# Even block: place of the values, order of the remainders and of the raw loads; third ffn: which down tile works on which state-space table

## The chip, the cores and the metric

The kernel runs on 1 core of one Trainium2 chip. The metric is the device time of that core in microseconds (us), for one execution of the whole program. Its engines are TensorE (PE, matmuls), VectorE (DVE), ScalarE (ACT), GpSimd (POOL) and SyncE (SP, here a queue that only starts DMAs). ScalarE starts some DMAs too. Each engine runs its own instructions strictly in the order of the program, and waits at semaphores for the others.

## The reference, cut to what matters

Two layers (DEPTH 2) of a hybrid network over 256 latent tokens and 256 context tokens, model width 1024, float32. Each layer is three stages, each closed by a layer norm with a scaled residual: a half ffn (SwiGLU, hidden width 2816), a mixer, and another half ffn.

```python
for l in range(DEPTH):
    x = half_ffn(x, mod_l, 0, ffn_a, ...);  cx = half_ffn(cx, mod_c, 0, ffn_a, ...)
    if l % 2 == 0:   # [2-D neighbourhood attention | bidirectional mLSTM]
        yc, yl = even_mixer(hc @ ev_w_in[e], hl @ ev_w_in[e], ...)
    else:            # [bidirectional S5 (state space) | bidirectional retention]
        yc, yl = odd_mixer(hc @ od_w_in[e], hl @ od_w_in[e], ...)
    x = layer_norm(alpha * x + gate(mod_l, 1) * (yl @ w_out), ...)
    x = half_ffn(x, mod_l, 2, ffn_b, ...)
```

The state-space part of the odd mixer needs, from the parameters alone, for each of 8 batches (4 groups of state tiles, 2 directions): operators (small input, output and local matrices) and tables, over the chunks of time, of sine, cosine and decay.

## The kernel before

The stages are ffn0, even block, ffn1, ffn2, odd block, ffn3. "The third ffn" is ffn2. Activations lie with the feature on the partition, 8 tiles of 128 features, 512 tokens wide (256 context, then 256 latent).

**High and low parts.** Most projections are done with rounded operands in three groups of matmuls: high weights by high inputs, high weights by low inputs, and low weights by high inputs. ScalarE makes the high part (a copy that rounds), VectorE the low part or remainder (weights minus high part).

**Even block, projections.** The first four tiles (input of the convolution) are followed by 21 parts, `PARTS`: 0 to 4 are the output gate (four) and the gate rows (part 2), 5 to 8 the queries, 9 to 12 the keys, 13 to 16 the attention's values, 17 to 20 the mLSTM's values. High parts lie in two buffers (`part_hi`, part u in u % 2): `next_hi(u)` on ScalarE makes the high part of u + 2 when TensorE has done part u. `part_rest(u)` (L2267) on VectorE makes the remainder. TensorE does a part in `even_tile` (L864, L866, then L869 with the remainder) or `even_values` (L885, L886, L890).

**State-space operators in the even block.** Between the parts TensorE also works for the odd block: `turn_raw(b)` (L798) transposes raw operands of batch b behind the parts of `TURN_BEHIND`, `s5_operators(b)` (L810, L813) turns and multiplies its blocks behind the parts of `OPERATORS_BEHIND`. VectorE's `s5_operators(b)` (L2186 to L2236) builds the input block (ready at L2224, semaphore s5_blk_ready) and the output block (L2234). ScalarE's `s5_operators(b)` (L1442) issues the raw loads of batch b + 2 (`raw_in`, L1439 and L1440, two buffers), copies the results out of PSUM (L1450, L1451, L1458) and issues two stores of operators to DRAM (L1462, L1464). After every second batch VectorE sums the local matrices (`s5_local_sum`, L2250, L2253) and ScalarE stores them (`local_out`, L1469). `REST_BEFORE` says which remainders VectorE makes in front of its work on batch b. The operators' work buffers are in slot 3 (`in_out`, `pre_tmp`), in `R` (`out_blk`, `local`) and in `L`. The mLSTM's values `ml_v` lie in slot 3 over `in_out`, so ScalarE waits for all stores (semaphores s5_ops_written, s5_local_written) before it copies them there (L1555).

**The gate rows.** ScalarE's `soft_rows` (L1517 to L1521) works behind part 4; VectorE then does scans over the rows (L2302 to L2318), and only behind these `part_rest(6)`.

**Attention.** TensorE transposes the rows (L923), forms scores two tiles at a time (L940), VectorE takes maxima (L2343 to L2347), ScalarE exponentials (`exps(p)`, L1590), VectorE scales (L2358), TensorE turns the probabilities (L969), ScalarE copies them (L1601). The third and fourth buffers of probabilities lie in `R`, over `local` and `out_blk`.

**Down tiles of an ffn.** TensorE does 8 output tiles (L711, L717, L720, for each of two halves of the weights). For tile d + 1 ScalarE makes the high parts (L1295; half 0 after half 0 of tile d, half 1 after tile d), VectorE the remainders (L2071). VectorE adds the residual of tile d (L1944), ScalarE squares it (L1325), GpSimd sums both (L2557, L2563). TensorE starts tile d + 2 only after the residual of tile d. At tile 7 the context and the latent tokens are done apart, and `norm_stats` (L750 to L758) needs the sums and the last residual and square (L1965, L1346).

**Tables in the third ffn.** For table u VectorE computes phases (`phases(u)`, L1778 to L1785), ScalarE two sines (`sines(u)`, L1266, L1267), GpSimd decay and cosine (`cosines(u)`, L2681 to L2686), and ScalarE stores the table (`table_out`, L1274). Two buffers, so `phases(u)` waits for the store of table u − 2. Before, table d belongs to down tile d, and each engine does it first thing in its step d.

Of the kernel before, what the change touches and what calls it, by code (L numbers as in the profile page):

```python
# [66 lines left out]
OPERATORS_BEHIND = {7: 0, 9: 1, 11: 2, 12: 3, 14: 4, 16: 5, 17: 6, 19: 7}  # L67
REST_BEFORE = {0: (7,), 1: (8, 9), 2: (10, 11), 3: (12,), 4: (13, 14), 5: (15, 16), 6: (17,), 7: (18, 19)}

# [7 lines left out]
BATCH = 4  # L77
BATCHES = [(k, way) for k in range(S5_TILES // BATCH) for way in range(2)]
TWO_PI = 2 * math.pi
ROUND = 1.5 * 2.0 ** 23  # L80
# [29 lines left out]
def build(nc, i, out, stop=None):  # L110

    stack = contextlib.ExitStack()
    with stack:
# [172 lines left out]
        VCOLS = HDIM + 1  # L286
        ml_v = slots[3][:, 1024:1024 + TT * HEADS * VCOLS].rearrange("p (t h n) -> p t h n", h=HEADS, n=VCOLS)
        na_q, na_k, na_v = view(R, 6144, 4, T), view(R, 8192, 4, T), view(slots[0], 0, TT, WIDTH)
# [882 lines left out]
        def _(act):  # L1171
# [91 lines left out]
            def sines(u):  # L1263

                act.wait_ge(sem("phase_ready"), u + 1)
                nc.scalar.activation(tables_out[:, u % 2, 1, :], phase[:, u % 2, :], ACT.Sin, scale=TWO_PI).then_inc(sem("phase_sin"), 1)  # L1266
                nc.scalar.activation(tables_out[:, u % 2, 0, :], phase[:, u % 2, :], ACT.Sin, scale=math.pi).then_inc(sem("phase_sin"), 1)  # L1267
                if u:
                    table_out(u - 1)

# [43 lines left out]
            def squares(name, c0):  # L1314

                for d in range(KT - 1):
                    if name == "ffn2":
                        sines(d)
                    if name[:3] == "ffn":
                        for half in range(2):  # L1320
                            down_weights_hi(int(name[3]), d + 1, half)
                    act.wait_ge(sem("r_ready"), before("r_ready", name) + d + 1)
                    if d >= 2:
                        act.wait_ge(sem("sums"), before("sums", name) + 2 * (d - 1))
                    nc.scalar.activation(sq[:, d % 2, c0:T], h[:, d, c0:T], ACT.Square).then_inc(sem("sq"), 1)  # L1325
                    if name == "ffn0" and d == 3:
                        parameters()
                    if name == "ffn0" and 2 <= d < 6:
                        first_tile_hi(d - 2)
                if name == "ffn2":  # L1330
                    sines(KT - 1)
                    table_out(KT - 1)

# [108 lines left out]
            def s5_operators(b):  # L1442

                k, way = BATCHES[b]
                act.wait_ge(sem("s5_blk_turned"), b + 1)
                if b + 2 < len(BATCHES):
                    raw_in(b + 2)
                if b >= 2:
# [23 lines left out]
            def even():  # L1472
# [57 lines left out]
                for u, (what, k, j) in enumerate(PARTS):  # L1530
# [5 lines left out]
                    elif what in ("na_v", "ml_v"):  # L1536
                        if j < 3:
                            quarters += 1
                            act.wait_ge(sem("even_quarter_done"), quarters)
                            next_hi(u)  # L1540
                        else:
                            if what == "ml_v":
                                local_out(3)
                                for b in range(2):
                                    act.wait_ge(sem(f"s5_ops_written{b}"), 32 * (len(BATCHES) // 2))
                                act.wait_ge(sem("s5_local_written"), 16 * (len(BATCHES) // 2))
                            for t in range(TT):
                                projected("even", n, k)
                                if t == TT - 1:
                                    next_hi(u)  # L1550
                                src = banks[t][:, :]
                                if what == "na_v":
                                    nc.scalar.activation(na_v[:, t, :], src, ACT.Copy).then_inc(read, 1)
                                else:
                                    nc.scalar.activation(ml_v[:, t, :, 0:HDIM], src.rearrange("p (h n) -> p h n", n=HDIM), ACT.Copy).then_inc(read, 1)  # L1555
                                n += 1
# [16 lines left out]
                    if u in OPERATORS_BEHIND:  # L1573
                        b = OPERATORS_BEHIND[u]
                        if b in (2, 4, 6):
                            local_out(b // 2 - 1)
                        s5_operators(b)
                act.wait_ge(sem("even_acol_done"), 1)
                nc.scalar.activation(acol[:, :, :, :].rearrange("p a b c -> p (a b c)"), banks[6][:, 0:2 * TT * HEADS], ACT.Copy).then_inc(sem("even_acol_ready"), 1)
# [23 lines left out]

                exps(0)
                for p in range(NA_PAIRS):
                    if p + 1 < NA_PAIRS:
# [126 lines left out]
        def _(dve):  # L1733
# [314 lines left out]
            def ffn(s):  # L2048
# [70 lines left out]
                for d in range(KT):  # L2119
                    if s == 2:  # L2120
                        phases(d)
                    if d + 1 < KT:
                        for half in range(2):
                            down_weights_lo(d + 1, half)
                    k = 3 + d % 2
                    slot_done[k] += 1
# [128 lines left out]
            def even():  # L2255
# [43 lines left out]
                part_rest(4)  # L2299
                part_rest(5)  # L2300
                dve.wait_ge(sem("even_soft"), 2)
                link(nc.vector.scalar_tensor_tensor(rows[:, 2:4, :], rows[:, 2:4, :], 0.0, rows[:, 6:8, :], ALU.min, ALU.subtract))  # L2302
# [8 lines left out]

                scans(4, 2, ALU.add)
                nc.vector.tensor_tensor(rows[:, 0:2, :], rows[:, 0:2, :], rows[:, 4:6, :], ALU.subtract).then_inc(sem("even_rows_step"), 1)
                dve.wait_ge(sem("even_rows_step"), 2)
# [3 lines left out]
                nc.vector.tensor_scalar(rows[:, 4:6, :], rows[:, 6:8, :], -1.0, None, ALU.mult)  # L2318
                part_rest(6)

                dve.wait_ge(sem("odd_params_in"), 16 * 6)
                for b in range(len(BATCHES)):
# [3 lines left out]
                    if b in (2, 4, 6):  # L2326
                        s5_local_sum(b // 2 - 1)
                part_rest(20)
                s5_local_sum(3)
# [216 lines left out]
        def _(pool):  # L2546
            def sums(name, c0):

                w = slice(c0, T)
                for d in range(KT - 1):  # L2550
                    if name == "ffn2":
                        cosines(d)
                    pool.wait_ge(sem("r_ready"), before("r_ready", name) + d + 1)
# [10 lines left out]
                    pool.wait_ge(sem("sums"), before("sums", name) + 2 * d + 2)  # L2564
                if name == "ffn2":
                    cosines(KT - 1)

# [28 lines left out]
            def even():  # L2596
# [14 lines left out]
                for k in range(1, len(BATCHES) // 2):  # L2611
                    pool.wait_ge(sem("s5_local_written"), 16 * k)
                    nc.gpsimd.memset(R[:, 12288:12800], 0.0).then_inc(sem("s5_zero"), 1)
                pool.wait_ge(sem("s5_local_written"), 16 * (len(BATCHES) // 2))
                for b in range(2):
                    pool.wait_ge(sem(f"s5_ops_written{b}"), 32 * (len(BATCHES) // 2))
                nc.gpsimd.memset(ml_v[:, :, :, HDIM:VCOLS], 1.0).then_inc(sem("ml_ready"), 1)
                nc.gpsimd.memset(outside, 0.0).then_inc(sem("s5_zero"), 1)
# [198 lines left out]
```

## Time and profile before

| what | value |
|---|---|
| median of 3 runs | 2010.73 us (2009.46 to 2012.52) |
| the profiled execution | 2010.62 us, span 2008.9 us |
| TensorE (PE) busy | 1876.0 us, 93% |
| VectorE (DVE) busy | 1296.9 us, 65% |
| ScalarE (ACT) busy | 675.5 us, 34% |
| GpSimd (POOL) busy | 300.6 us, 15% |
| mean granted TensorE clock | 0.963 of full |
| chain that ended last | PE 78%, DVE 13%, DMA 4%, ACT 4% |

The span is the time between the first and the last record of the profiled execution. The chain is followed back from the last instruction to what released it, step by step. The even block's parts run from about 450 to 619 us, its attention to about 690; the third ffn's down tiles run from 1444.9 to 1581.5 us.

### The profile page before, as it was taken

How to read it: one execution, taken by the hardware profiler on the slowest of the kernel's cores; microseconds unless marked ns; L12 is line 12 of the kernel's file. 1: busy time of each engine (PE TensorE's matmuls, PEld its weight loads, DVE VectorE, ACT ScalarE, POOL GpSimd, SP SyncE). 2: the span in 40 equal slices, each digit the busy share in tenths (PEclk: the TensorE clock that was granted, in tenths of full speed). 3: DMA queues.
4: the chain of work that ended last, by engine and by line, in shares of the span. 5: the costliest groups of instructions: out<-in, count | busy, mean ns of one | idle time of the engine just before them, and what ended most of it. 6: DMA issues, size and time to landing. Idle time of an engine off the chain costs nothing.

```text
span 2008.9 us, 24713 instructions
## 1 busy us (share of the span) xinstructions
PE 1876.0 (93%) x9400; PEld 1544.3 (77%) x9400; DVE 1296.9 (65%) x2254; ACT 675.5 (34%) x1139; POOL 300.6 (15%) x321
## 2 busy tenths in 40 slices
PE   5999999997996789899999989999999899989997
PEld 5888877896873455688887878888778867879997
DVE  7677776766984572877778357774677534465464
ACT  2322242344544431422224233222423232324453
POOL 0000001144000003400000231000045435130002
PEclk7999999998997899899999999999999999989999
DMA  9354544215431101354544233544134544214443
GB/s 359 124 199 185 187 163 164 93 55 126 151 138 68 43 1 42 147 203 174 199 159 175 87 153 124 197 182 151 79 118 191 220 188 176 84 43 168 171 167 123
DMA packets 43960, 290.13 MB, mean 144 GB/s; under 512 B 13916, under 2 KB 19676, under 8 KB 27232
## 3 DMA queue, kind: packets, MB, share of 16 engines
q1 hardware_dynamic: 35488, 271.13, 36.6%
q10 hardware_dynamic: 8384, 17.83, 2.3%
q8 instruction: 56, 0.92, 0.2%
q14 instruction: 32, 0.26, 0.0%
HBM read 272.16 MB, written 16.78 MB: 144 GB/s over the span
## 4 chain that ended last, share of the span: by engine, by line
PE 78%; DVE 13%; DMA 4%; ACT 4%; issue 1%; POOL 0%; SPq 0%; ACTq 0%; POOLq 0%; DVEq 0%
PE bank L654 13%; PE bank L659 13%; PE bank L656 13%; PE bank L711 6%; PE bank L720 5%; PE bank L717 5%; PE bank L1061 2%; PE bank L778 2%; DMA R<-in_ada_dram 2%; PE bank L768 1%; PE bank L1058 1%; DMA slot<-in_down_dram 1%; PE bank L825 1%; DVE g_lo L2077 1%; PE bank L869 1%
## 5 line engine op out<-in xcount | busy, mean ns | idle before, releaser
L1856 DVE CUSTOM_DVE_ANT_0 L<-slot 128x1024 f32<-128x1024 f32 x272 | 337.7, 1242 | 82.5 <-DMA slot<-in_ada_dram 75.3
L1245 ACT ACTIVATE w_hi<-slot 128x1024 fp32r<-128x1024 f32 x176 | 186.3, 1060 | 572.5 <-PE bank L659 561.2
L1904 DVE TENSOR_TENSOR w_lo<-slot,w_hi 128x1024 fp32r<-128x1024 f32 x176 | 217.0, 1235 | 210.2 <-ACT w_hi L1245 203.5
L654 PE MATMUL bank<-m_hi,w_hi 128*128 128x512 f32 (+1 forms) x1344 | 296.6, 363 | 3.2 <-ACT w_hi L1245 3.2
L659 PE MATMUL bank<-m_hi,w_lo 128*128 128x512 f32 (+1 forms) x1344 | 296.1, 362 | 0.0
L656 PE MATMUL bank<-m_lo,w_hi 128*128 128x512 f32 (+1 forms) x1344 | 296.1, 362 | 0.0
L654 PEld LDWEIGHTS bank<-m_hi,w_hi 128*128 128x128 f32 x1344 | 232.3, 189 | 43.1 <-ACT w_hi L1245 4.0
L659 PEld LDWEIGHTS bank<-m_hi,w_lo 128*128 128x128 f32 x1344 | 232.6, 189 | 39.3
L656 PEld LDWEIGHTS bank<-m_lo,w_hi 128*128 128x128 f32 x1344 | 232.6, 189 | 39.2
L2071 DVE TENSOR_TENSOR down_lo<-slot,down_hi 128x1408 fp32r<-128x1408 f32 x64 | 107.9, 1699 | 122.0 <-ACT down_hi L1295 121.8
L717 PE MATMUL bank<-g_lo,down_hi 128*128 128x512 f32 (+1 forms) x770 | 155.8, 350 | 0.1
L717 PEld LDWEIGHTS bank<-g_lo,down_hi 128*128 128x128 f32 x770 | 127.6, 192 | 19.5 <-DVE g_lo L2077 1.0
L1295 ACT ACTIVATE down_hi<-slot 128x1408 fp32r<-128x1408 f32 x64 | 87.6, 1377 | 155.4 <-PE bank L720 109.2
L2555 POOL COPY L<-h 128x512 f32<-128x512 f32 (+1 forms) x6 | 3.6, 605 | 897.7 <-DVE h L1944 897.7
L711 PE MATMUL bank<-g_hi_mid,down_hi 128*128 128x512 f32 (+1 forms) x420 | 99.7, 368 | 1.8 <-ACT g_hi_mid L1305 1.5
L720 PE MATMUL bank<-g_hi_mid,down_lo 128*128 128x512 f32 (+1 forms) x420 | 89.4, 349 | 0.0
L711 PEld LDWEIGHTS bank<-g_hi_mid,down_hi 128*128 128x128 f32 x420 | 72.4, 195 | 20.1 <-ACT g_hi_mid L1305 9.8
L720 PEld LDWEIGHTS bank<-g_hi_mid,down_lo 128*128 128x128 f32 x420 | 70.2, 192 | 9.9
L2557 POOL TENSOR_TENSOR L<-L,h 128x512 f32<-128x512 f32 (+1 forms) x36 | 43.6, 1212 | 223.0 <-DVE h L1944 222.4
L1325 ACT ACTIVATE L<-h 128x512 f32<-128x512 f32 (+1 forms) x42 | 23.5, 561 | 138.1 <-DVE h L1944 135.2
L2576 POOL TENSOR_TENSOR h<-h,L 128x256 f32<-128x256 f32 x79 | 62.8, 830 | 38.2 <-DVE L L1973 38.2
L678 PE MATMUL bank<-m_hi,w_hi 128*128 128x256 f32 x112 | 37.9, 355 | 25.2 <-ACT m_hi L1219 22.5
(374 smaller groups left out, 2792.8 us busy)
## 6 DMA issues: line engine op xcount, KB each, us to landing
slot<-in_gateup_dram SPq DMA_DIRECT2D x44, 2048.0 KB, 7.9
slot<-in_ada_dram SPq DMA_DIRECT2D x34, 2048.0 KB, 7.9
slot<-in_down_dram SPq DMA_DIRECT2D x32, 1408.0 KB, 6.2
slot<-in_ev_in_dram SPq DMA_DIRECT2D x4, 2048.0 KB, 9.0
slot<-in_od_in_dram SPq DMA_DIRECT2D x4, 2048.0 KB, 9.8
R<-s_ops SPq DMA_DIRECT2D x16, 512.0 KB, 6.3
s_tables<-slot ACTq DMA_DIRECT2D x8, 768.0 KB, 3.3
R<-s_tables SPq DMA_DIRECT2D x8, 768.0 KB, 6.3
```

The lines of the kernel that those rows point to most:

```text
L654: nc.tensor.matmul(bank[j][:, c0:T], w_hi[:, off, c, :], m_hi[:, c, c0:T], start=(c == 0), stop=False)
L656: nc.tensor.matmul(bank[j][:, c0:T], w_hi[:, off, c, :], m_lo[:, c, c0:T], start=False, stop=False)
L659: last = nc.tensor.matmul(bank[j][:, c0:T], w_lo[b][:, 2 * j + off, c, :], m_hi[:, c, c0:T], start=False, stop=(c == KT - 1))
L711: nc.tensor.matmul(out_d, down_hi[:, half, f % HALF, :], g_hi(f)[:, a:b], start=(f == 0), stop=False)
L717: nc.tensor.matmul(out_d, down_hi[:, half, f % HALF, :], g_lo[:, f, a:b], start=False, stop=False)
L720: last = nc.tensor.matmul(out_d, down_lo[k - 3][:, half, f % HALF, :], g_hi(f)[:, a:b], start=False, stop=(f == FT - 1))
L1245: nc.scalar.activation(w_hi[:, off, :, :].rearrange("p a b -> p (a b)"), slots[b][:, (2 * (f % 2) + off) * D:(2 * (f % 2) + off + 1) * D], ...
L1295: nc.scalar.activation(down_hi[:, half, :, :].rearrange("p a b -> p (a b)"), slots[k][:, half * HALF * P:(half + 1) * HALF * P], ACT.Copy) ...
L1856: ins = nc.vector.tensor_tensor_reduce(out=junk, in0=slots[k][:, t * D:(t + 1) * D], in1=csilu[s_], scale=1.0, scalar=0.0, op0=ALU.mult, o ...
L1904: nc.vector.tensor_tensor(w_lo[b][:, t, :, :].rearrange("p a b -> p (a b)"), slots[b][:, t * D:(t + 1) * D], w_hi[:, off, :, :].bitcast(F3 ...
L2071: nc.vector.tensor_tensor(down_lo[d % 2][:, half, :, :].rearrange("p a b -> p (a b)"), slots[3 + d % 2][:, half * HALF * P:(half + 1) * HA ...
L2576: nc.gpsimd.tensor_tensor(h[:, d, a:b], h[:, d, a:b], mean[:, a:b], ALU.subtract).then_inc(sem("c"), 1)
```

## The change

In the even block: `ml_v` moves from slot 3 into `R`, over the low feature tiles of the projections' inputs. Its copies need no wait for stores; that wait now stands between `exps(0)` and `exps(1)` on ScalarE. `local_out(3)` is issued after the loop over the parts. `part_rest(6)` is made before the soft rows are waited for, `part_rest(7)` behind the first scans, and each batch of operators has the remainders of one part further in front of it. The raw loads of batch b + 2 are issued at the end of the part before batch b's, as soon as VectorE's input block of b is ready. In the third ffn: the tables are worked on at down tiles 0 to 5, two at each of the first two (`TABLES_AT`); on VectorE the phases come behind one or both remainders, on ScalarE the sines behind both high parts, and the stores one tile later behind the first high part.

```diff
@@ constants
-REST_BEFORE = {0: (7,), 1: (8, 9), 2: (10, 11), 3: (12,), 4: (13, 14), 5: (15, 16), 6: (17,), 7: (18, 19)}
+REST_BEFORE = {0: (8,), 1: (9, 10), 2: (11, 12), 3: (13,), 4: (14, 15), 5: (16, 17), 6: (18,), 7: (19, 20)}
+TABLES_AT = [(0, 1), (2, 3), (4,), (5,), (6,), (7,), ()]
...
-        ml_v = slots[3][:, 1024:1024 + TT * HEADS * VCOLS].rearrange("p (t h n) -> p t h n", h=HEADS, n=VCOLS)
+        ml_v = R[:, 13312:13312 + TT * HEADS * VCOLS].rearrange("p (t h n) -> p t h n", h=HEADS, n=VCOLS)
@@ ScalarE
-                if u:
-                    table_out(u - 1)
...
                 for d in range(KT - 1):
-                    if name == "ffn2":
-                        sines(d)
                     if name[:3] == "ffn":
                         for half in range(2):
                             down_weights_hi(int(name[3]), d + 1, half)
+                            if name == "ffn2" and d and half == 0:
+                                for u in TABLES_AT[d - 1]:
+                                    table_out(u)
+                    if name == "ffn2":
+                        for u in TABLES_AT[d]:
+                            sines(u)
...
-                if name == "ffn2":
-                    sines(KT - 1)
-                    table_out(KT - 1)
...
                 act.wait_ge(sem("s5_blk_turned"), b + 1)
-                if b + 2 < len(BATCHES):
-                    raw_in(b + 2)
...
-                            if what == "ml_v":
-                                local_out(3)
-                                for b in range(2):
-                                    act.wait_ge(sem(f"s5_ops_written{b}"), 32 * (len(BATCHES) // 2))
-                                act.wait_ge(sem("s5_local_written"), 16 * (len(BATCHES) // 2))
...
                         s5_operators(b)
+                    if OPERATORS_BEHIND.get(u + 1, len(BATCHES)) + 2 < len(BATCHES):
+                        act.wait_ge(sem("s5_blk_ready"), OPERATORS_BEHIND[u + 1] + 1)
+                        raw_in(OPERATORS_BEHIND[u + 1] + 2)
+                local_out(3)
                 act.wait_ge(sem("even_acol_done"), 1)
...
                 exps(0)
+                act.wait_ge(sem("s5_local_written"), 16 * (len(BATCHES) // 2))
+                for b in range(2):
+                    act.wait_ge(sem(f"s5_ops_written{b}"), 32 * (len(BATCHES) // 2))
@@ VectorE
                 for d in range(KT):
-                    if s == 2:
-                        phases(d)
                     if d + 1 < KT:
                         for half in range(2):
                             down_weights_lo(d + 1, half)
+                            if s == 2:
+                                for u in TABLES_AT[d]:
+                                    if (d == 0 or u != TABLES_AT[d][0]) == (half == 1):
+                                        phases(u)
...
                 part_rest(4)
                 part_rest(5)
+                part_rest(6)
                 dve.wait_ge(sem("even_soft"), 2)
...
                 scans(4, 2, ALU.add)
+                part_rest(7)
...
-                part_rest(6)
...
-                part_rest(20)
                 s5_local_sum(3)
@@ GpSimd
                     if name == "ffn2":
-                        cosines(d)
+                        for u in TABLES_AT[d]:
+                            cosines(u)
...
-                if name == "ffn2":
-                    cosines(KT - 1)
...
+                pool.wait_ge(used[1], uses_before("even")[1] + 3)
+                nc.gpsimd.memset(ml_v[:, :, :, HDIM:VCOLS], 1.0).then_inc(sem("ml_ready"), 1)
                 pool.wait_ge(sem("s5_local_written"), 16 * (len(BATCHES) // 2))
-                for b in range(2):
-                    pool.wait_ge(sem(f"s5_ops_written{b}"), 32 * (len(BATCHES) // 2))
-                nc.gpsimd.memset(ml_v[:, :, :, HDIM:VCOLS], 1.0).then_inc(sem("ml_ready"), 1)
```

## Rows read from the trace of the kernel before

**Rows 1.** waits of TensorE in the even block: who it waited for, total, times, longest.
```profile
PE bank L869 <- DVE w_lo L2267: 11.7, 1, 11.7
PE bank L923 <- ACT slot L1555: 10.6, 1, 10.6
PE bank L798 <- DMA L<-in_s_c_dram: 3.4, 1, 3.4
```

**Rows 2.** waits of TensorE from the third ffn's down tiles into the odd block.
```profile
PE bank L758 <- ACT L L1346: 3.5, 1, 3.5
PE bank L711 <- ACT down_hi L1295: 3.1, 1, 3.1
PE bank L756 <- DVE h L1965: 1.6, 1, 1.6
```

**Rows 3.** timeline of VectorE, first operator batch: start, length, line, operation, count.
```profile
490.05 1.21 DVE L2302 SCALAR_TENSOR_TENSOR slot<-slot 4x1024 f32<-4x1024 f32 x1 [11.16 <-ACT slot L1521]
...
500.20 2.34 DVE L2267 TENSOR_TENSOR w_lo<-slot,part_hi 128x1024 fp32r<-128x1024 f32 x2
...
506.66 1.26 DVE L2224 TENSOR_TENSOR L<-slot 64x192 f32<-64x192 f32 x4
```

**Rows 4.** chain that ended last, 500 to 640 us: start, length, what.
```profile
501.46 3.78 PE bank L869 x8
...
510.90 0.88 PE bank L810 x8
511.78 1.71 PE bank L813 x16
...
517.21 1.81 PE bank L869 x8
```

**Rows 5.** timeline of ScalarE around the first operator batch.
```profile
510.94 1.06 ACT L1491 ACTIVATE part_hi<-slot 128x1024 fp32r<-128x1024 f32 x1 [4.06 <-PE bank L869]
...
514.78 0.60 ACT L1450 ACTIVATE slot<-bank 128x512 f32<-128x512 f32 x1 [2.24 <-issue]
...
517.87 0.83 ACT L1458 ACTIVATE R<-bank 32x128 f32<-32x128 f32 x3
```

**Rows 6.** the same chain, at the end of the even projections.
```profile
608.44 8.09 DMA s_local<-R
```

**Rows 7.** timeline of the SyncE queue, same stretch.
```profile
608.28 0.33 SPq L428 DMA_DIRECT2D slot<-in_ev_out_dram  x1
```

**Rows 8.** timeline of VectorE in the attention, second pair of tiles.
```profile
629.46 0.15 DVE L2355 RECIPROCAL col<-col 128x2 f32<-128x2 f32 x1
```

**Rows 9.** TensorE by stretch: sum, busy (instructions), granted clock, DMA share, GB/s.
```profile
555.00:560.00 5.00, 1.65 (x9) 1.00 0.93 356
619.00:625.00 6.00, 5.22 (x28) 0.50 0.00 0
...
1573.00:1578.00 5.00, 5.00 (x28) 0.57 0.15 60
```

**Rows 10.** timeline of VectorE in the third ffn's down tiles.
```profile
1458.54 0.69 DVE L1778 TENSOR_TENSOR slot<-shared,s_turn 128x512 f32<-128x512 f32 x1
...
1462.97 0.43 DVE L1785 TENSOR_SCALAR slot<-slot 128x512 f32<-128x512 f32 x1
...
1487.43 1.67 DVE L1780 TENSOR_TENSOR slot<-slot 128x512 f32<-128x512 f32 x1
```

**Rows 11.** timeline of ScalarE, same tiles.
```profile
1464.49 2.63 ACT L1295 ACTIVATE down_hi<-slot 128x1408 fp32r<-128x1408 f32 x2
1470.95 0.63 ACT L1325 ACTIVATE L<-h 128x512 f32<-128x512 f32 x1 [3.83 <-DVE h L1944]
```

**Rows 12.** timeline of GpSimd, same tiles.
```profile
1466.79 1.87 POOL L2686 TENSOR_SCALAR slot<-slot 128x512 f32<-128x512 f32 x1
```

**Rows 13.** chain that ended last, third ffn, one of six groups of a tile.
```profile
1481.24 2.49 PE bank L711 x11
```

**Rows 14.** instructions that touch the table buffer in DRAM: landing times.
```profile
DMA to landing us min/median/max: 3.2/3.3/3.6
```

## The prediction, made before the changed kernel ran

> **What bounds the kernel now.** I read the page first: TensorE is busy 93% of the span, so only its waits are to be had. Then its waits, stretch by stretch. In the even block three waits sum to 25.7 us: 11.7 for a remainder (L2267), 3.4 for raw operands, 10.6 for the values' copies (L1555) [rows 1]. In the third ffn they are 3.1 at the second down tile and 3.5 + 1.6 at the context statistics [rows 2]. Then the queues behind each. VectorE's `part_rest(6)` stands after the scans, which start at 490.05 when the soft rows come, and runs from 500.20 with `part_rest(7)`; the first block of operators is ready at 507.9 [rows 3]. TensorE loses more than the wait: the L869 group behind it takes 3.78 us [rows 4], against 1.82 for a later one. The values wait for a 256 KB store that took 8.09 us and ended at 616.5 [rows 6]; it shares the DMA engines with the 2 MB load issued at 608.28 [rows 7].
>
> **Even block, the first batch.** Now `part_rest(6)` needs only its high part, there long before 490, and `part_rest(7)` fits behind the first scans. So TensorE ends part 6 at 491.6 and part 7 at 497.1. But batch 0 needs its block, and VectorE does the same scans and two remainders (7 and 8) before it: ready at 508.0, as before. The 11 us wait moves to batch 0. TensorE was there at 510.90 before [rows 4], so it is 2.9 us ahead, less the 2.0 that slow matmuls cost behind such a wait (3.78 − 1.82), which were within the 510.90 before and now come after it: **−0.9**.
>
> **Even block, later batches.** This is the step that decides. The remainder in front of batch b is now that of the part after the one that TensorE does before the batch. Its high part can be made only when the part two earlier is done (two buffers). So from the end of part u−1: 1.1 for the high part [rows 5], 1.2 for the remainder (half of 2.34), 5.4 from the end of the remainders (502.5) to the end of the block's last operation (507.9) [rows 3], and small gaps: 7.85. TensorE needs for part u 5.5 (from the end of the L813 row, 513.49, to the end of the last row, 519.03) and mostly a turn of 0.2 [rows 4]: 5.7. It waits 2.1 at batches 1, 2, 4, 5 and 7: 10.5. Batch 7 waits 0.8 more, since ScalarE copies batch 6 (3.9, 514.78 to 518.70 [rows 5]) ahead of part 20's high half. Batches 3 and 6 follow a batch with one part between: VectorE needs 3.0 for output blocks, 1.2 and 5.4, after batch 2 also 1.8 for the local sum; TensorE 2.6 (the L810 and L813 rows) and 5.5. Waits: 3.4 and 1.6. Turns 3 and 6 wait 1.0 and 0.8 for ScalarE's copies, which come later as batches do. ScalarE's new wait for the block (in front of the raw operands) has the next high part and copies queued behind it; they are within these figures. Sum **+18.1**. Bounds: 0, were VectorE ahead by then; 24 with 3.4 at each of seven. I take 18.1, as VectorE is idle between remainder and high part by this count and cannot get ahead.
>
> The sooner raw operands save the 3.4 at turn 5: batch 3's block is ready before the 2 MB value load of slot 1 has ended, but the part in between hides the rest: **−3.4** (bound: 0).
>
> **Values.** The copies no longer wait for the stores. They end 0.6 after part 20, where they ended 10.6 after: **−10.0**. The wait for the stores goes in front of the second pair of exponentials. The store goes out 0.6 after part 20's slot is free and meets the same load; with 8.1 us it lands some 8.7 after part 20. VectorE first wants that pair's sums for the reciprocal at 629.46 [rows 8], 10.7 after the copies end (618.8), and until then it forms the next maxima; so the wait is hidden, and without that cover it costs up to 4. TensorE also goes into attention without an 11 us pause: between 619 and 625 its granted clock was 0.50, in place of 1.00 [rows 9]. Six microseconds at half speed hold 5.2 of TensorE work, of which 2.6 could go; the pair that waits for the store takes some back: **−1.7** (bounds 0 and −2.6). Even block: −0.9 + 18.1 − 3.4 − 10.0 − 1.7 = **+2.1**.
>
> **Third ffn, start.** A set of phases is 4.9 us alone (1458.54 to 1463.40) [rows 10]. It went before tile 1's weights; now it goes behind both remainders of them. So the 3.1 goes, and tile 0 ends at 1462.9. But the first two phases now start only after that: high half to 1464.5, remainder to 1466.1, phases to 1471.0, and the second set to 1477.4 (1.5 added, since GpSimd's cosines of the first run beside it). Then the residual 0.9, the square 0.6 and the high half 1.3 for tile 2 [rows 11], gaps 0.5: tile 2 starts at 1480.7, where TensorE was ready at 1477.9. Before it started at 1481.2 [rows 13]; a tile is six such groups, 14.96. Next, table 0 goes out at 1480.7. A table lands in 3.3 [rows 14], but a down load (1408 KB, 6.2 on the page) left at 1477.9; so between 1484 and 1487, I take 1485.5. Phases to 1490.4, remainder to 1492.0, the second set with GpSimd beside it to 1498.9 (+2.0), residual, square, high half: 1502.2. TensorE was ready for tile 3 at 1495.7; before it started at 1496.2. That is a 6.5 wait and a lag of 6.0; the clock may add 0 to 2.2, I take 1.0. With one table a tile after that the lag stays: **+7.0** (bounds +4.5 and +9.5).
>
> What GpSimd beside VectorE costs: L1780 took 1.67 where the like L1778 took 0.69 [rows 10]: 1.0, and two such make the +2.0. GpSimd's L2686 took 1.87 beside a remainder [rows 12], where its shortest is 0.62: it loses 1.2. The Trainium skill (SBUF — State Buffer, "SBUF: two separate sides") says that the pair of ports is locked for the whole instruction and the loser fully blocks. The rows show both sides longer at once. By that rule each doubled set would lose the cosines' whole 2.7 (two of 1.04 and one of 0.62) in place of my 1.5 and 2.0, tile 3 would lag 1.9 more, and the sum would be 2014.3, an estimate by that page.
>
> **Third ffn, end.** No tables stand before the last square and residual: the 3.5 and 1.6 go. Behind them the clock was at 0.57 for 5 us [rows 9]: 2.15 lost. In the second ffn, which has no tables, TensorE runs straight through this place. **−7.3**. Third ffn: +7.0 − 7.3 = **−0.3**.
>
> **Sum.** The profiled execution took 2010.62 (span 2008.9; median of three 2010.73): 2010.62 + 2.1 − 0.3 = **2012.4 us**. 0.2% is 4.0 us, about what a measurement here can tell from none.
>
> **Rivals.** (A) Operators do not gate: VectorE has the blocks ready, the 18.1 vanish, 1994.3. For it speaks that it never gated before; against it, that a remainder then needed a part one older. Chance 0.12. (B) The doubled tables are hidden, by faster stores or less overlap: −3.1 in place of +7.0, as tile 1 starts sooner: 2002.3. Against it: two sets are 9.8 of a tile's 15.0 and ScalarE's next high half is queued behind their sines. 0.13. (C) Slower: the clock falls behind the batches' waits too. Behind a single 3.4 wait it was 1.00 [rows 9], behind 1.6 + 3.5 close together 0.57; waits of 2 to 3 with small tiles between may be like the second. At 2.15 each, two make 2016.7 and decide; four make 2021.0. 0.30. (D) The forecast, 0.45, own range 2008 to 2017; the part of it over 2014.7 is about a quarter.
>
> **Numbers.** Range 2003 to 2021: it leaves out A and the tail of C. Faster 0.12 + 0.13 = 0.25; slower 0.30 and a quarter of 0.45, 0.41; same the rest, 0.34.
>
> **What would show it.** TensorE waits at L810 for VectorE L2224, once 11 us and seven times 2 to 3; no wait at L869; L923 waits under 1 us; L711 waits twice in the third ffn, some 3 and 6 us, with none at L758. Wrong if L810 doesn't wait, if exponentials wait past the maxima, or if tile 3 starts on time.

## The result, and the profile after

The changed kernel takes **2031.17 us**, median of 4 (2030.63 to 2032.07), where the kernel before, run beside it, took 2011.62 (2009.46 to 2013.02): ratio 1.0099, 95% interval 1.0081 to 1.0116. It is slower by 19.6 us, and outside the forecast's range of 2003 to 2021. The profiled execution took 2031.47 (span 2029.7, mean granted clock 0.957), 20.85 above that of before.

First the waits of TensorE, in the even block and in the third ffn, as [rows 1] and [rows 2] had them (line numbers after are one or two higher: L811, L814, L886 and L924 were L810, L813, L885 and L923):

```profile
PE bank L811 <- DVE L L2226: 25.9, 8, 10.7
PE bank L799 <- ACT R L1456: 1.3, 2, 0.9
PE bank L924 <- ACT R L1548: 0.9, 1, 0.9
...
PE bank L712 <- ACT down_hi L1294: 8.2, 2, 5.7
```

The wait for part 7's remainder and the 10.6 at the rows' transposes are gone, and the operators' block is waited for eight times, as forecast: 10.7 once, and 15.2 in the seven others (I had 16.3). Up to the end of the 21 parts the waits sum to 27.2 us, before to 15.1: +12.1. But part 20's last group of matmuls starts at 635.46 where it started at 606.27: +29.2. The other 17.1 are in no wait. The windows of TensorE show them (sum, busy, granted clock, DMA share, GB/s):

```profile
core 0: us, PE busy (x) PEld busy (x) DVE busy (x) ACT busy (x) POOL busy (x), PEclk, DMA share, GB/s
508.00:520.00 12.00, 12.00 (x44) 10.55 (x45) 4.06 (x9) 5.39 (x15) 0.00 (x0) 0.58 0.30 109
520.00:550.00 30.00, 25.75 (x138) 21.21 (x138) 21.53 (x72) 12.09 (x23) 0.00 (x0) 1.00 0.35 123
550.00:570.00 20.00, 16.92 (x71) 14.45 (x70) 10.69 (x35) 9.29 (x27) 0.53 (x1) 0.74 0.72 263
578.00:590.00 12.00, 11.12 (x54) 9.29 (x53) 6.22 (x14) 5.79 (x14) 0.52 (x1) 0.86 0.34 126
606.00:615.00 9.00, 8.71 (x38) 7.93 (x39) 6.14 (x15) 1.90 (x5) 0.53 (x1) 0.62 0.08 29
626.00:637.00 11.00, 11.00 (x47) 9.51 (x47) 4.61 (x13) 4.51 (x14) 0.00 (x0) 0.69 0.24 95
```

and two windows of before:

```profile
500.00:520.00 20.00, 18.54 (x86) 15.46 (x87) 19.43 (x65) 7.93 (x19) 0.00 (x0) 0.86 0.14 51
550.00:570.00 20.00, 16.65 (x87) 13.84 (x86) 15.15 (x57) 7.46 (x19) 0.53 (x1) 1.00 0.56 209
```

A stretch of t us at clock c loses t x (1 - c). The windows of the changed kernel with a clock under 1.00 lose 5.0, 5.2, 1.7, 3.4 and 3.4 us, together 18.7. Before, the clock was 0.86 in 500 to 520 (2.8 lost) and 1.00 between 520 and 590. The difference is 15.9 of the 17.1 that the waits leave over. The windows also take in some idle time at a lower clock, so I count by rows too. A batch and the part behind it, up to the part's last group (L891), take 6.36 us behind the wait of 1.62, and 10.86, 7.98, 9.79 and 9.60 behind those of 3.08, 2.09, 2.18 and 2.36. With 0.14 off the first and the third of these four, for a turn that stands in between, they cost 12.5. The first batch and its part cost 2.9 more than the slow groups of before. That is 15.4; the other 1.7 are in small gaps. The stretches end while TensorE works on: in narrower windows the clock is 0.55 from 557 to 567 and 1.00 from 567 to 570. The same instructions behind a wait at either level of the clock, and the last group of the part behind the first batch, from the timeline of TensorE:

```profile
519.12 2.01 PE L870 MATMUL bank<-even_m_hi,w_lo 128*128 128x512 f32 x8
...
528.92 1.09 PE L811 MATMUL bank<-ident,L 128*128 128x128 f32 x8 [2.08 <-DVE L L2226]
529.85 1.87 PE L814 MATMUL bank<-L 128*128 128x32 f32 x16
...
556.78 1.97 PE L811 MATMUL bank<-ident,L 128*128 128x128 f32 x8 [3.08 <-DVE L L2226]
558.54 3.46 PE L814 MATMUL bank<-L 128*128 128x32 f32 x16
...
606.29 1.41 PE L811 MATMUL bank<-ident,L 128*128 128x128 f32 x8 [2.18 <-DVE L L2226]
607.49 3.46 PE L814 MATMUL bank<-L 128*128 128x32 f32 x16
```

Sixteen small matmuls take 1.87 us at full clock (2.4 GHz) and 3.46 at half (1.2 GHz). Behind 2.08 us of waiting the clock stayed here, behind 2.18 it fell; that is no threshold, as the run of the even block alone shows below.

Behind part 20, from the timeline of TensorE:

```profile
638.33 1.13 PE L924 MATMUL bank<-ident,slot 4*128 4x4 f32 x16 [0.88 <-ACT R L1548]
639.39 1.15 PE L941 MATMUL bank<-R 64*128 64x256 f32 x8
```

and from the chain that ended last and the timelines of ScalarE and VectorE:

```profile
637.50 8.22 DMA s_local<-R
...
645.74 0.47 ACT L1587 ACTIVATE R<-bank,col 128x256 f32<-128x256 f32 x1 [4.06 <-DMA s_local<-R]
...
647.67 0.15 DVE L2357 RECIPROCAL col<-col 128x2 f32<-128x2 f32 x1
```

The row transposes come at 638.33 where they came at 618.90: +19.4, so the values' 10.6 us have shrunk by 9.8. The store took 8.22 us (8.09 in [rows 6]), but most of it now passes beside the attention's first pair of tiles. The reciprocal of [rows 8] comes 18.2 later, and ffn1's first matmul at 833.09 instead of 813.69, so the whole even block is **+19.4**.

The third ffn, from the chain and the windows. Tile 3 starts at the L712 row:

```profile
1497.87 8.37 DMA s_tables<-slot
1506.27 0.69 DVE slot L1778
...
1522.53 5.03 PE bank L712 x11
```
```profile
1522.00:1532.00 10.00, 9.47 (x29) 7.61 (x30) 8.97 (x10) 2.21 (x3) 6.04 (x4) 0.67 0.39 157
1532.00:1540.00 8.00, 8.00 (x37) 6.60 (x36) 6.03 (x5) 2.61 (x4) 6.61 (x5) 1.00 0.24 98
```

Tile 0 ends 19.65 us later than before. Tile 3 starts at 1522.53, 26.3 later, so it has lost 6.7 more; its first group then takes 5.03 instead of 2.49, behind a 5.7 us wait. The waits at the statistics are gone. From the first matmul of tile 0 to the first of the odd block (L826) it takes 140.3 us (1464.53 to 1604.84), before 138.3 (1444.90 to 1583.20): **+2.0** for the third ffn. 19.4 + 2.0 leave about -0.6 for the rest.

### The profile page after: what moved, and what is told of

Same layout as the page of the kernel before. It is cut to its first block, busy times and chain, and to the rows that moved or that the text cites. A ratio compares the mean times of both kernels' runs of the same rounds, so it can differ in the third digit from the quotient of the medians.

```text
span 2029.7 us, 24718 instructions
## 1 busy us (share of the span) xinstructions
PE 1894.2 (93%) x9400; PEld 1557.6 (77%) x9400; DVE 1291.2 (64%) x2254; ACT 674.8 (33%) x1139; POOL 296.8 (15%) x321
## 4 chain that ended last, share of the span: by engine, by line
PE 74%; DVE 15%; ACT 4%; DMA 4%; issue 2%; SPq 0%; ACTq 0%; POOL 0%; POOLq 0%; DVEq 0%
PE bank L655 13%; PE bank L660 13%; PE bank L657 13%; PE bank L712 6%; PE bank L721 5%; PE bank L718 5%; PE bank L1062 2%; PE bank L779 2%; DVE L L1856 1%; PE bank L769 1%; PE bank L1059 1%; DMA slot<-in_down_dram 1%; PE bank L826 1%; PE bank L1017 1%; DVE h L1992 1%
## 5 line engine op out<-in xcount | busy, mean ns | idle before, releaser
L712 PE MATMUL bank<-g_hi_mid,down_hi 128*128 128x512 f32 (+1 forms) x420 | 102.2, 374 | 1.9 <-ACT g_hi_mid L1304 1.5
L712 PEld LDWEIGHTS bank<-g_hi_mid,down_hi 128*128 128x128 f32 x420 | 73.9, 199 | 21.0 <-ACT g_hi_mid L1304 10.1
```

Of the source, the lines that this page charges most:

```text
L712: nc.tensor.matmul(out_d, down_hi[:, half, f % HALF, :], g_hi(f)[:, a:b], start=(f == 0), stop=False)
```

## The experiments

### Remainders back behind the scans

```diff
-REST_BEFORE = {0: (8,), 1: (9, 10), 2: (11, 12), 3: (13,), 4: (14, 15), 5: (16, 17), 6: (18,), 7: (19, 20)}
+REST_BEFORE = {0: (), 1: (8, 9), 2: (10, 11), 3: (12,), 4: (13, 14), 5: (15, 16), 6: (17,), 7: (18, 19)}
...
+                part_rest(20)
                 s5_local_sum(3)
```

The changed kernel, but from batch 1 on each batch has the remainders ahead of it that it had before; parts 6 and 7 stay around the scans.

> The changed kernel with REST_BEFORE one part back (batch 0 has no remainder in front, 1 has 8 and 9, 2 has 10 and 11, ...), the rest of the change kept. Theory 1 (the batches' waits cost their own length and, in addition, matmuls at half clock behind them): TensorE's seven waits of 1.6 to 3.1 us at L811 behind the first (15.2 us in all) vanish but perhaps one of 2.5 at batch 7, and so do the slow stretches (some 14 us); the wait at batch 0 is 10 in place of 10.7. Time 2001 to 2005. Theory 2 (the waits cost their own length only, the rest of the loss is in attention or the third ffn): 2017 to 2019, with the granted clock between 520 and 637 us still under 0.9.

2000.43 us (1999.49 to 2003.02), ratio to before 0.9951 (0.9934 to 0.9967), 0.6 below the range that I expected. TensorE's waits and its windows:

```profile
PE bank L811 <- DVE L L2226: 9.6, 1, 9.6
PE bank L799 <- DMA L<-in_s_c_dram: 2.0, 1, 2.0
```
```profile
508.00:520.00 12.00, 12.00 (x50) 10.25 (x51) 11.63 (x37) 6.65 (x18) 0.00 (x0) 0.78 0.38 124
520.00:550.00 30.00, 30.00 (x172) 25.90 (x171) 25.42 (x82) 17.33 (x41) 0.57 (x1) 1.00 0.54 196
550.00:570.00 20.00, 17.97 (x94) 14.94 (x93) 16.51 (x59) 7.76 (x21) 0.53 (x1) 1.00 0.55 212
578.00:590.00 12.00, 12.00 (x67) 10.29 (x67) 11.40 (x38) 8.41 (x25) 0.53 (x1) 1.00 0.32 127
```

The seven waits are gone and the clock is 1.00 from 520 to the end of the parts. The one place further for the remainders costs the changed kernel 31 us, twice the seven waits that it makes; without it the rest of the change is a gain.

### TensorE kept at work in front of the batches' waits

```diff
-                pe.wait_ge(sem("s5_blk_ready"), b + 1)
                 if b:
                     pe.wait_ge(sem("s5_in_read"), b)
+                    for f in range(7):
+                        nc.tensor.matmul(banks[4][:, :], even_m_hi[:, f, 0:P], even_m_hi[:, f, :], start=True, stop=True)
+                pe.wait_ge(sem("s5_blk_ready"), b + 1)
```

Seven matmuls whose result nobody reads, before each of the seven later waits; the wait for the block itself moves behind them.

> The changed kernel with 7 matmuls of 128x512 (their results unused, into a bank that is free then) in front of TensorE's wait at each batch from 1 to 7: 1.6 us of work where TensorE stood for 1.6 to 3.1 us. Output unchanged. Theory 1 (half clock behind the waits is what was missed): the clock stays at or near 1.00 from 520 to 637 us, part 20 ends 8 to 14 us sooner, the time is 2018 to 2023. Theory 2 (the clock is not the cause, the matmuls behind the waits are slow for another reason): no gain, 2031 to 2033.

2028.85 us (2025.28 to 2029.91), ratio to before 1.0085 (1.0068 to 1.0101). Windows and waits (L813 is L811 here):

```profile
520.00:550.00 30.00, 28.31 (x150) 23.42 (x149) 21.28 (x72) 12.08 (x23) 0.00 (x0) 1.00 0.35 124
550.00:570.00 20.00, 17.16 (x90) 14.06 (x89) 14.11 (x46) 9.89 (x27) 0.53 (x1) 1.00 0.72 263
578.00:590.00 12.00, 10.35 (x47) 8.26 (x47) 6.17 (x22) 4.72 (x13) 0.53 (x1) 1.00 0.28 109
606.00:615.00 9.00, 9.00 (x41) 7.42 (x41) 3.32 (x5) 4.73 (x13) 0.53 (x1) 1.00 0.37 146
```
```profile
PE bank L813 <- DVE L L2228: 16.3, 6, 10.7
PE bank L799 <- ACT R L1458: 2.7, 2, 1.7
PE bank L799 <- DMA L<-in_s_c_dram: 1.3, 1, 1.3
```

The clock is 1.00 in each of these windows, where it was 0.74, 0.86 and 0.62 in three of them. That shows that the idle time brings the clock down, and that the slow stretches are no other feature of the batches. The last stretch (610 to 640) stays slow, 0.83 where the changed kernel has 0.82: there TensorE still waits 2.76 us behind its filler, while the longest of its waits for a block since the first batch is 1.52. The gain was 2.3 us where I expected 8 to 13, since the filler is no free cover: it is busy for 12.2 us itself, and filler and waits together sum to 32.5 us, 5.3 more than the 27.2 of waits. Part 20 still ends 5.3 us sooner (its last group starts at 630.12, not 635.46), so some 10.6 us of slow clock were recovered. The 0.63 of 508 to 520 stays: the first wait, of 10.7, had no filler.

### The even block alone, and each of its three edits alone

The changed even block with the tables as before:

> The changed even block alone; the third ffn's tables as before. By the traces the even block costs 19.4 of the 20.8 us of span, and the third ffn 1.9: 2029 to 2031. If instead the two parts of the change act on each other (loads that start sooner or later), it is off this by more than 2 us.

2031.64 us (2031.18 to 2032.00), ratio to before 1.0101 (1.0084 to 1.0118), 0.6 above the range that I expected: the even block alone makes the whole loss. By its profile the third ffn takes 138.2 us, as before and 2.1 less than in the changed kernel, but the even block comes out longer: ffn1 starts at 834.57, not 833.09. The block's instructions are the same, and the slow stretches lie elsewhere. The clock is 0.67 from 530 to 540, behind a wait of 2.10 us, where the changed kernel had 1.00 behind 2.08, and 1.00 from 606 to 615, where the changed kernel had 0.62. So the tables' +2.0 is the trace's figure; the times of the two kernels can't tell it from nothing.

The kernel before with one edit each. The values:

```diff
-        ml_v = slots[3][:, 1024:1024 + TT * HEADS * VCOLS].rearrange("p (t h n) -> p t h n", h=HEADS, n=VCOLS)
+        ml_v = R[:, 13312:13312 + TT * HEADS * VCOLS].rearrange("p (t h n) -> p t h n", h=HEADS, n=VCOLS)
...
                 exps(0)
+                act.wait_ge(sem("s5_local_written"), 16 * (len(BATCHES) // 2))
+                for b in range(2):
+                    act.wait_ge(sem(f"s5_ops_written{b}"), 32 * (len(BATCHES) // 2))
...
```

> The kernel before with the values' move alone: ml_v in R, its wait for the local store and the operator stores behind the first exponentials, the remainders, the raw operands and the tables as before. As predicted for this part (-10.0, less the 4 us that ScalarE waits inside the attention in the changed kernel, if those show): 2001 to 2003 us. Rival, the store's wait only moves to the second pair of exponentials and most of it comes back there: 2005 to 2009 us.

2002.11 us (2001.13 to 2005.95), ratio 0.9953 (0.9936 to 0.9969), some 9.5 us faster, as expected.

The remainders (`REST_BEFORE` of the change, parts 6 and 7 around the scans, no `part_rest(20)` at the end):

> The kernel before with the remainders' move alone (parts 6 and 7 around the scans, one part more ahead of every batch), values, raw operands and tables as before. Theory 1 (each batch's operators gate TensorE, 15 us of waits, and behind the waits the granted clock falls, another 13 to 16 us): 2036 to 2041 us, part 20 ends near 636, the granted clock of 0.6 to 0.8 in stretches between 550 and 637. Rival (the waits need the sooner raw operands or the moved values as well): 2011 to 2028 us with a clock of 1.00.

2035.89 us (2028.13 to 2038.52), ratio 1.0120 (1.0103 to 1.0137). Its profiled execution is the shortest of the four (span 2026.4). Its waits and two windows:

```profile
PE bank L810 <- DVE L L2224: 23.4, 6, 10.7
PE bank L923 <- ACT slot L1555: 3.4, 1, 3.4
```
```profile
550.00:570.00 20.00, 18.05 (x81) 14.72 (x80) 12.57 (x49) 9.41 (x26) 0.52 (x1) 0.84 0.69 260
578.00:590.00 12.00, 9.86 (x44) 7.57 (x42) 5.91 (x24) 6.94 (x17) 0.53 (x1) 1.00 0.36 130
```

The remainders alone make the waits and bring the clock down, though in this profile less than in the changed kernel's, and the runs spread over 10 us. That the spread comes from the clock isn't shown: the mean granted clocks of the four executions, from the fastest to the slowest, are 0.959, 0.958, 0.959 and 0.964. The values' wait is 3.4 here in place of 10.6. The parts run so late that the local store goes out at 631.02, ahead of the 2 MB load of 632.38, and takes 2.35 us, where before it went out behind that load and took 8.09.

So the edits don't add. Medians of these three runs alone, with 10.5 and 1.0 off for the values and the raw operands and 23.3 on for the remainders, would make 2024.4 us; the changed even block takes 2031.64, 7.2 more, and the values' wait had shrunk by 7.2 already. The values' move is worth 10 us in the kernel before, but at most 3.4 once the remainders are late.

The raw operands (`raw_in(b + 2)` at the end of the part before batch b's):

> The kernel before with the sooner raw operands alone. As predicted for this part, TensorE's wait for the last batch's operands (3.4 us) goes and nothing else moves: 2007 to 2009 us. Rival, the block then waits elsewhere for the same end (the local store's chain): 2010.5 to 2012 us.

2011.63 us (median of 10, 2006.91 to 2012.76), ratio 0.9993 (0.9983 to 1.0003), 1.4 us faster and 3.4 at the most: nothing that can be told, as the rival had it; the span of its profile is 2008.8, of before 2008.9. Its waits of TensorE:

```profile
PE bank L923 <- ACT slot L1553: 11.3, 1, 11.3
PE bank L798 <- DMA L<-in_s_c_dram: 0.9, 1, 0.9
```

The turn's 3.4 is down to 0.9, and 0.7 of it is back in front of the values, which wait for the store: 10.6 has become 11.3.

### The tables: one a tile, doubled at the fifth

```diff
-TABLES_AT = [(0, 1), (2, 3), (4,), (5,), (6,), (7,), ()]
+TABLES_AT = [(0,), (1,), (2,), (3,), (4, 5), (6,), (7,)]
```

and a tile's first table between the two remainders at tile 0 too, the last store behind the tiles.

> The changed kernel with the tables placed otherwise: one at each of the down tiles 0 to 3, two at tile 4, one at 5 and 6, the first of a tile always between the two remainders (tile 0 too), the last stored behind the loop. Theory 1 (two sets in the first two tiles delay the next tile's high half; the store of table 0 makes it worse): waits at L712 for down_hi go, the third ffn takes 3.1 + 7.3 less than before the change, so 9 to 12 us less than in the changed kernel: 2019 to 2022. Rival (any doubled tile costs a wait and a slow stretch): one wait of 2 to 6 us at tile 5 or 6 stays, 2024 to 2028.

2023.27 us (2021.33 to 2025.05), ratio to before 1.0060 (1.0043 to 1.0077), 7.9 below the changed kernel, and between the two ranges that I had given. TensorE's waits in the third ffn:

```profile
PE bank L751 <- POOL L L2569: 2.2, 1, 2.2
```

Both waits for the weights' high half are gone. What remains, 2.2 at the statistics, stands behind GpSimd's last cosine. By the profile the third ffn takes 129.6 us, 10.7 less than in the changed kernel and 8.7 less than before; 1.8 of this are lost again in its even block, where ffn1 starts at 834.87 and not at 833.09. So the doubled first tiles cost what the end had given, and the end's gain was real.

### Both together, and three attempts at the rest

> The changed kernel with the remainders back behind the scans (as the run with the remainders back) and the tables one a tile, doubled at the fifth (as the run with that alone). If the two add: 2000.4 - 8 = 1992 us, 1990 to 1995. Rival, they overlap (the third ffn's waits for the weights' halves were partly made by the state that the slower even block left): 1996 to 2000 us.

**1992.07 us** (1991.03 to 1992.56), ratio 0.9899 (0.9883 to 0.9916). The two add up: 8.4 below the run with the remainders back, where the tables alone gave 7.9.

Third and fourth score buffers in slot 3, so that the store isn't waited for inside the attention:

> The run with the remainders back and the tables one a tile, and besides the third and fourth score buffers in slot 3 instead of R, so that the second pair of exponentials waits for the operator stores alone and the wait for the local store stands behind the attention. If ScalarE's wait of 4.1 us in there is on the path: 1988 to 1989.5 us. Rival, the operator stores land no sooner, or VectorE's softmax work catches up with it later: 1991 to 1993 us.

1989.39 us (1987.14 to 1994.96), ratio 0.9896 (0.9876 to 0.9915), not to be told from 0.9899. ScalarE's wait for the store (4.4 us in the run without this edit) is gone, but over the attention TensorE waits 3.4 us for VectorE's scaled scores in those buffers, where it waited 1.4, and 2.8 for the raw operands instead of 2.0; its own 2.3 behind that pair's exponentials are gone. If anything came of it, it is less than these runs can tell.

Doubled tables at the fourth and fifth tiles, none at the last:

> The run with the remainders back and the tables one a tile, but the doubled tables at the fourth and fifth tiles and none at the last, so that GpSimd's last cosine is not in front of the sums: TensorE's wait of 2.2 us at the statistics goes, 1989.5 to 1990.5 us. Rival, the doubled tables on VectorE and ScalarE make the weights' halves late again, as in the first tiles of the changed kernel: 1993 to 1998 us.

1996.91 us (1995.22 to 1998.17), ratio 0.9927 (0.9911 to 0.9944): the rival.

```profile
PE bank L721 <- DVE down_lo L2074: 3.6, 1, 3.6
PE bank L712 <- ACT down_hi L1294: 3.4, 1, 3.4
```

The 2.2 at the statistics goes and 7.0 of waits for the weights' halves come, 4.8 net. By the profiles the third ffn takes 7.8 us more than without this edit (137.4, not 129.6); the other 3.0 weren't traced step by step, but the clock is 0.75 from 1540 to 1550, behind the 3.6 wait, which is 2.5 of them. The medians differ by 4.8. A single doubled tile, as the fifth above, has a slack that two in a row haven't, in the middle of the stage or at its start.

> The two runs before this one together: 1986 to 1988 us if each is worth its wait (4.1 and 2.2 us), 1992 if neither is.

1995.08 us (1994.11 to 1996.64), ratio 0.9918 (0.9901 to 0.9934), above both figures that I had given. The doubled middle tiles lose again, and the buffers' move, 1.8 us below the run without it, is again not to be told from nothing.

## Why the prediction was wrong

It had slower as the likeliest side, and its own figure near no change, 1.8 us over the profiled 2010.62; the size was wrong: 2012.4 against a profiled 2031.5. Step by step:

- **First batch.** Forecast: TensorE at 497.1, block ready at 508.0, 11 us of waiting. Measured 10.7, block at 507.92: the wait was right. The slow stretch behind it was sized at 2.0 and was 5.0 (0.58 over 508 to 520). So the step came out at +2.1 and not at -0.9: the last group of the part behind it starts at 519.12, in the same view before at 517.05.
- **Later batches' waits.** Forecast 16.3 in seven (2.1 five times, one of them with 0.8 more, 3.4, 1.6) and 1.8 at the turns. Measured 15.2 and 1.3. The count of the remainder's chain from the end of part u - 1 was right, and with the remainders back the seven waits were gone.
- **The step that failed** is in the same place, the +18.1 of the later batches: the waits were summed at their own length. The clock behind them was priced at nothing in the forecast and left to rival C, at 2.15 each for two or four of them. It fell at four of the seven: 5.2, 1.7, 3.4 and 3.4 us, 13.7 in all by the windows and 12.5 by the rows. Part 20's last group came 15.4 later than the +13.8 forecast: 12.5 by this clock, 3.0 by the first batch, 1.5 by small gaps, less 1.6 since the waits were a little shorter than forecast. Rival C had the mechanism and the direction; its worst case (2021.0) still fell 10 us short. Some 4 to 5 of these are its price: 2.15 was read from one stretch of 5 us [rows 9], while here one stretch lasted 10 us. The others are the first batch, the attention and the third ffn. The row used against it, a single 3.4 us wait with a clock of 1.00 behind it, was true of that one execution. At the same place the run with the values' edit alone waits 2.98 us, and its clock is 0.82 from 555 to 560 and 0.84 from 560 to 565; in the run with the buffers moved the wait there is 2.79 and the clock 0.83 from 550 to 560. So it isn't shown that the waits must come in a row: each is a chance of a slow stretch, and the edit made seven.
- **Raw operands.** Forecast -3.4. Alone, the edit gave 1.4 or nothing: 2.5 us of the turn's wait went, and 0.7 of it was waited for again in front of the values. Where the other 1.8 went was not traced.
- **Values.** Forecast -10.0, measured -9.8 against before and about -9.5 alone: right. But the forecast added it to late remainders as if they didn't touch it; with these alone only 3.4 of the wait is left. The faster clock (forecast -1.7) came: the first eight score matmuls took 1.15 us, not the 2.08 of before, and the second pair's reciprocal was 1.2 closer than the transposes had been. But by ffn1 this was given back, 19.4 again: attention waits for VectorE and ScalarE where TensorE is fast, and ScalarE stood 4.06 us for the store. Which of these took it is open.
- **Third ffn, start.** Tile 3's lag was forecast at 6.0 and was 6.7; the table's store, taken as landing 4.8 us after its issue, took 8.37, beside a down load, but had been issued 2.5 sooner than by my count. Its slow clock cost 3.1 (18.05 for the tile, not 14.96) instead of 1.0. **End:** the waits went as forecast; what is left for it is -7.8 against -7.3. Sum +2.0 against -0.3.
- **GpSimd beside VectorE.** Forecast +1.5 and +2.0 for two sets of phases. In the second of the two, in front of tile 3, L1778 and L1779 took 1.53 instead of 0.69 and L1780 0.98: +2.0; the sizes were right. The reading of the rows that the prediction set against the rule was not. From the timelines of VectorE and GpSimd:

```profile
1512.58 1.53 DVE L1778 TENSOR_TENSOR slot<-shared,s_turn 128x512 f32<-128x512 f32 x1
1514.03 1.53 DVE L1779 TENSOR_TENSOR slot<-shared,s_turn 128x512 f32<-128x512 f32 x1
1515.59 0.98 DVE L1780 TENSOR_TENSOR slot<-slot 128x512 f32<-128x512 f32 x1
```
```profile
1512.46 1.09 POOL L2681 TENSOR_TENSOR slot<-s_rho,shared 128x512 f32<-128x512 f32 x1 [9.19 <-ACT slot L1268]
1513.52 1.49 POOL L2684 TENSOR_TENSOR slot<-slot 128x512 f32<-128x512 f32 x1
1515.10 0.94 POOL L2686 TENSOR_SCALAR slot<-slot 128x512 f32<-128x512 f32 x1
```

Each took its own time and, less some 0.15 us, what was left of the other engine's instruction when it started. L1778: 0.69 and the 0.97 until L2681 ends at 1513.55, 1.66 against 1.53. L2684: 1.04 and the 0.59 until L1778 ends, 1.63 against 1.49. The next three fit as well (1.67, 1.08 and 1.14 against 1.53, 0.94 and 0.98). So the two engines took turns, instruction by instruction, and a record's length holds the wait; they weren't slow at once. By the exclusive lock of the Trainium skill (SBUF — State Buffer, "SBUF: two separate sides") the one that starts first keeps the shared ports for its whole instruction and the other waits; the trace agrees. The prediction's estimate by that page, 2.7 lost by VectorE in each set, was too much because GpSimd waits too, and VectorE waits only for what is left.

The differences sum up: even block 17.3 (15.4 up to part 20, 1.9 behind it), third ffn 2.3, the rest -0.6: 19.0 of 2031.5 - 2012.4 = 19.1.

## What to carry to other kernels

A wait of TensorE of 2 to 3 us can cost more than its length: after summing the waits that an edit brings, price slow stretches behind them too (here 13.7 us on top of 15.2), and don't take one wait with a full clock behind it in one profile as evidence against it. When one queue makes both what is needed now and what the next step needs, count what a move in it does to every later turn of the loop, not only to the first. Check too whether one edit changes what another is worth: late parts had already hidden 7 of the values' 10 us. Here doubled work in one tile was absorbed when the tiles behind it were single; two doubled tiles in a row cost 10.7 us at the start of the stage and 7.8 in its middle.

## What the runs showed of the hardware

Behind waits of 2.18, 2.36 and 3.08 us, in a loop with a wait every 10 to 20 us, TensorE ran at half clock for up to 10 us, and behind one of 2.09 for some 3.4; behind those of 2.08, 1.75 and 1.62 in the same loop it stayed at 1.00. In another run of the same block the clock fell behind a wait of 2.10 (0.67 from 530 to 540). A wait that stood alone did either: 1.00 behind 3.35 us before, 0.82 around one of 2.98 with the values' edit alone. Seven dummy matmuls in front of each wait kept it at 1.00 from 520 to 615 us, though not at the last batch, where 2.76 us of waiting were left. What decides between waits of nearly one length stays open. A 768 KB store, issued 0.3 us behind a 1408 KB load, took 8.37 us, where such a store took 3.2 to 3.6 before [rows 14]. A 256 KB store took 2.35 us ahead of a 2 MB load and 8.09 behind one. GpSimd and VectorE instructions with two 128x512 inputs each, issued side by side, ran in turn: 1.49 us instead of 1.04 and 1.53 instead of 0.69.
